# Opening of a one-core transformer kernel: four weight units in one table, split by k, and a shorter run of ones products

## The chip, the cores and the metric

One core of one Trainium2 chip runs the whole kernel. The metric is the device time of one execution in microseconds (us). The kernel before takes 1102.69 us, the median of 3 runs (1102.63 to 1103.09).

## The reference, cut to what matters

A batch of one sequence of 512 positions with 1024 channels goes through two blocks (a gated DeltaNet with retention and a gated MLP, then sliding-window attention with pooling and a long convolution). Only its first step matters here:

```
n = rms_norm(x, attn_norm_w)              # [512, 1024]
proj = n @ w_in                           # w_in is [1024, 4104], float32
gq, gk, gv, gg, ga, gb, rq, ... = split(proj)
```

The kernel works on transposed tiles: 128 channels on the partitions, 512 positions along the free axis. It multiplies x by the norm weight first and applies 1/rms to the products, so that the products needn't wait for the mean of the squares. The mean is needed once the first products are read out.

## The kernel before

**Products in three parts.** A float32 product is made of three float32r products, `w_hi x_hi + w_hi x_lo + w_lo x_hi` (`three`, L1912 to L1916). ScalarE makes the rounded part `hi` of a weight block (`split_hi`, L641 to L655), GpSimd makes the rest `lo = raw - hi` (`split_lo`, L531 to L535; for the very first blocks L545 to L549). Of x, ScalarE makes `hi` (`operand_hi`, L672), VectorE makes `lo` (`operand_lo`, L1223 to L1227).

**Units, halves and buffers.** The weights are taken in units of 128 output columns by all 1024 rows, that is 8 k-blocks of 128 rows. A unit is two halves of 4 k-blocks. The halves of units 0 to 3 are taken as a quad: halves n = 0 to 3 are the first halves (k 0 to 3) of the four units, n = 4 to 7 the second halves. `RAW` holds two slots of float32 weights, each a pair of units (8 k-blocks by 256 columns). `WH` and `WL` hold 4 halves each; half n lies in place n % 4, so half 4 can be written only when half 0 has been multiplied. The semaphore `half_done` says so. One k-block of one unit is 3 products of 128 rows by 512 columns; the four units are 96 of them, and unit 4 follows.

**Order of the opening, TensorE.** After four GpSimd memsets it makes 16 products of a table of ones with itself (L2092 to L2094), whose result nobody reads. Then `two_units` (L1964) runs four times: k 0 to 3 for units 0 and 1, k 0 to 3 for units 2 and 3, then k 4 to 7 for units 0 and 1, then for units 2 and 3. Ahead of the fourth, one float32 product of ones with the summed squares (`stat`, L2061 to L2064) gives the mean for the norm.

**Order of the opening, loads.** ScalarE's queue issues x tiles 0 and 1 (L693). SyncE's queue issues in this order (L382 to L400): norm weights; k 0 and 1 of the first pair of units (L383, 256 KB); k 2 and 3 (L384); x 2 and 3; k 0 to 3 of the second pair (L386, 512 KB); x 4 and 5; k 4 to 7 of the first pair (L388); x 6 and 7; k 4 to 7 of the second pair (L390); then the other parameters, the identity, the small a and b columns, the masks and the cosines. Weight rows are 1 KB long (256 columns), x rows 2 KB. Then the loop of L405 loads pair 2 once `free_slot(2)` holds, that is after 6 `lo` parts (L106 to L108 and L360).

**Order of the opening, ScalarE (L695 to L735).** `hi` of x 0, of weights k 0 and 1 for units 0 and 1 (L711), of x 1, of weights k 2 and 3 (L717), of x 2 and 3; squares of x 0 and 1; halves 2 and 3; x 4 and 5; squares 2 and 3; halves 4 and 5; x 6 and 7; squares 4 and 5; halves 6 and 7; squares 6 and 7; a table load; the two steps to 1/rms; halves 8 and 9.

**Order of the opening, VectorE (L1244 to L1262).** A product of two rows of norm weights (L1246); `lo` of x 0 to 3; sums of squares 0 and 1; `lo` of x 4 and 5; sums 2 and 3; `lo` of x 6 and 7; sums 4 to 7. Squares lie in two buffers in turn, so that square k waits for sum k - 2 (L676).

```
            pe.wait_ge(ones_ready, 4)                                  # L2092
            for _ in range(16):
                mm(PS[:, 7, 0:P], ONES[:, :], ONES[:, :], start=True, stop=True)
```

Of the kernel before, what the change touches and what calls it, by code (L numbers as in the profile page):

```python
# [9 lines left out]
P = 128  # L10
S = 512
D = 1024
KT = D // P
# [92 lines left out]
def split_when_free(p):  # L106

    return 4 * p - 2 if 2 * (p - 2) in QUADS else 4 * (p - 1)  # L108
# [12 lines left out]
def loads_before(p):  # L121

    n = 0
    for q in range(p % 2, p + 1, 2):
        n += 1 if q < 2 else 3 if U6 <= 2 * q < U7 else 2
    return n


def build(nc, a, const, out):
    ctx = ExitStack()  # L130
    with ctx:
# [9 lines left out]
        RAW = at("raw", [P, 2, KT, 256], F32, 0)  # L141
        WH = at("w_hi", [P, 4, 4, P], F32R, 16384)
# [145 lines left out]
        first_in = [sem("first_weights_in0"), sem("first_weights_in1")]  # L288
# [4 lines left out]
        head_in, head_hi, head_lo = sem("head_weights_in"), sem("head_hi_ready"), sem("head_lo_ready")  # L293
# [52 lines left out]
        def f32(ap):  # L346
            return ap.bitcast(F32)
# [7 lines left out]
        def _(sp):  # L355
# [22 lines left out]
            def x_tiles(k0):  # L378
                for k in (k0, k0 + 1):
                    sp.dma_start(XT[:, k, :], a["x"][:, k, :]).then_inc(x_in[k], 16)  # L380

            sp.dma_start(PAR[:, 0:88], a["params"][:, 0:88]).then_inc(par_in, 16)  # L382
            sp.dma_start(RAW[:, 0, 0:2, :], rows(w_in, 0, 2, 512)).then_inc(head_in, 16)  # L383
            sp.dma_start(RAW[:, 0, 2:4, :], rows(w_in, 2 * P, 2, 512)).then_inc(first_in[0], 16)  # L384
            x_tiles(2)
            sp.dma_start(RAW[:, 1, 0:4, :], rows(w_in, 0, 4, 768)).then_inc(first_in[1], 16)  # L386
            x_tiles(4)
            sp.dma_start(RAW[:, 0, 4:8, :], rows(w_in, 512, 4, 512)).then_inc(raw_in[0], 16)  # L388
            x_tiles(6)
            sp.dma_start(RAW[:, 1, 4:8, :], rows(w_in, 512, 4, 768)).then_inc(raw_in[1], 16)  # L390
# [122 lines left out]
        def raw_half(n):  # L513
# [5 lines left out]
            t = u % 2  # L519
            if by_heads(n):  # L520
                return r.rearrange("p k (v t d) -> p k v t d", v=2, t=2)[:, :, :, t, :]
# [8 lines left out]
        def _(gp):  # L530
# [96 lines left out]
        def _(act):  # L627
# [13 lines left out]
            def split_hi(n, i=None):  # L641
# [5 lines left out]
                if n < 4:  # L647
                    act.wait_ge(first_in[p], 16)
                elif i is None:
                    act.wait_ge(raw_in[p % 2], 16 * loads_before(p))  # L650
# [47 lines left out]
            def x_operands(k0):  # L698
                for k in (k0, k0 + 1):
                    act.wait_ge(x_in[k], 16)  # L700
                    operand_hi(XT[:, k, :], XA[:, k, 0, :], vec("attn_norm_w", k))

            def x_squares(k0):
                for k in (k0, k0 + 1):
                    square(0, k, XT[:, k, :], SC[:, 2 + k % 2, :])

            act.wait_ge(x_in[0], 16)
            operand_hi(XT[:, 0, :], XA[:, 0, 0, :], vec("attn_norm_w", 0))
            act.wait_ge(head_in, 16)
            for n in range(2):  # L710
                nc.scalar.activation(WH[:, n, 0:2, :], RAW[:, 0, 0:2, n * P:(n + 1) * P], ACT.Copy) \  # L711
                    .then_inc(head_hi, 1)
            act.wait_ge(x_in[1], 16)
            operand_hi(XT[:, 1, :], XA[:, 1, 0, :], vec("attn_norm_w", 1))
            act.wait_ge(first_in[0], 16)
# [1871 lines left out]
```

## Time and profile before

| | before |
|---|---|
| median of 3 runs | 1102.69 us |
| the profiled execution's own time | 1104.48 us |
| its span | 1102.60 us |
| TensorE busy (share of the span) | 1087.8 us (99%) |
| VectorE busy | 669.3 us (61%) |
| GpSimd busy | 501.0 us (45%) |
| ScalarE busy | 463.9 us (42%) |

The span runs from the first instruction to the last. The profiled execution's own time holds what lies around the span as well, 1.88 us. Its span is 0.09 us under the median. TensorE is busy all along, so what can be won on a stretch is only what TensorE idles or does for nothing in it. A float32 matmul on TensorE is recorded as two instructions, a float32r matmul as one.

### The profile page before, as it was taken

The numbers are of one execution on the slowest core, as the hardware profiler recorded it, in microseconds if no ns is written. First come the engines' busy times: TensorE is split into PE (matmuls) and PEld (weight loads), VectorE is DVE, ScalarE is ACT, GpSimd is POOL, SyncE is SP. The second block draws the span as 40 slices with busy tenths as digits, with TensorE's granted clock in tenths as the row PEclk, the third lists the DMA queues.
The fourth block names the chain that finished last, engine by engine and source line by source line (L and its number), as shares of the span: only waits on it lengthen the run. The fifth ranks groups of instructions, "written<-read, shape, count | busy, mean of one in ns | idle before, by whom it ended". The sixth has DMA issues, their size and how long they took to land.

```text
span 1102.6 us, 16181 instructions
## 1 busy us (share of the span) xinstructions
PE 1087.8 (99%) x5898; PEld 876.4 (79%) x5898; DVE 669.3 (61%) x967; ACT 463.9 (42%) x805; POOL 501.0 (45%) x375
## 2 busy tenths in 40 slices
PE   8999999999999999999999999999999999999997
PEld 7786878788788888888888888877778778888786
DVE  5875886416656666666641222558754757986863
ACT  6436422254744333333333334345464543243663
POOL 4446342122555444444454445433347686632451
PEclk9999999999999999999999999999999999999999
DMA  9952532151222323232322325322115222212222
GB/s 244 136 88 50 64 79 39 58 132 41 77 95 97 115 76 114 76 114 76 114 77 95 105 81 149 114 77 78 39 53 138 56 78 78 77 40 78 77 77 77
DMA packets 101722, 97.29 MB, mean 88 GB/s; under 512 B 4896, under 2 KB 95776, under 8 KB 101280
## 3 DMA queue, kind: packets, MB, share of 16 engines
q1 hardware_dynamic: 101232, 95.71, 31.7%
q8 instruction: 39, 0.64, 0.2%
q10 hardware_dynamic: 432, 0.79, 0.2%
q14 instruction: 19, 0.16, 0.0%
HBM read 94.38 MB, written 2.10 MB: 88 GB/s over the span
## 4 chain that ended last, share of the span: by engine, by line
PE 87%; DVE 7%; ACT 3%; issue 1%; DMA 1%; POOL 1%; SPq 0%; POOLq 0%; DVEq 0%; ACTq 0%
PE ps L1914 25%; PE ps L1916 24%; PE ps L1915 24%; PE ps L2455 4%; PE ps L2118 1%; DVE x_a L1226 1%; DMA raw<-in_w_in 1%; DVE conv L1758 1%; PE ps L2390 1%; PE ps L2401 1%; PE ps L2284 1%; DVE tt L1338 1%; ACT x_a L672 1%; PE ps L2378 1%; POOL w_lo L534 1%
## 5 line engine op out<-in xcount | busy, mean ns | idle before, releaser
L534 POOL TENSOR_TENSOR w_lo<-raw,w_hi 128x512 fp32r<-128x512 f32 (+1 forms) x330 | 447.1, 1365 | 569.5 <-ACT w_hi L655 558.7
L655 ACT ACTIVATE w_hi<-raw 128x512 fp32r<-128x512 f32 (+1 forms) x330 | 201.2, 620 | 254.5 <-PE ps L1916 238.3
L1914 PE MATMUL ps<-x_a,w_hi 128*128 128x512 f32 x624 | 252.2, 404 | 5.8 <-POOL w_lo L534 3.1
L1916 PE MATMUL ps<-x_a,w_lo 128*128 128x512 f32 x624 | 243.5, 390 | 0.0
L1915 PE MATMUL ps<-x_a,w_hi 128*128 128x512 f32 x624 | 243.4, 390 | 0.0
L1914 PE MATMUL ps<-x_b,w_hi 128*128 128x512 f32 x416 | 162.6, 391 | 0.0
L1916 PE MATMUL ps<-x_b,w_lo 128*128 128x512 f32 x416 | 161.9, 389 | 0.0
L1915 PE MATMUL ps<-x_b,w_hi 128*128 128x512 f32 x416 | 161.9, 389 | 0.0
L1914 PEld LDWEIGHTS ps<-x_a,w_hi 128*128 128x128 f32 x624 | 117.2, 188 | 41.0 <-issue 10.6
L1916 PEld LDWEIGHTS ps<-x_a,w_lo 128*128 128x128 f32 x624 | 117.2, 188 | 25.0
L1915 PEld LDWEIGHTS ps<-x_a,w_hi 128*128 128x128 f32 x624 | 117.3, 188 | 24.6 <-issue 2.2
L1914 PEld LDWEIGHTS ps<-x_b,w_hi 128*128 128x128 f32 x416 | 78.1, 188 | 17.5 <-issue 0.8
L1916 PEld LDWEIGHTS ps<-x_b,w_lo 128*128 128x128 f32 x416 | 78.1, 188 | 16.3
L1915 PEld LDWEIGHTS ps<-x_b,w_hi 128*128 128x128 f32 x416 | 78.1, 188 | 16.2 <-issue 0.2
L1758 DVE TENSOR_TENSOR conv<-ps,conv 32x511 f32<-32x511 f32 (+2 forms) x96 | 65.5, 682 | 17.2 <-ACT conv L1100 14.4
L1916 PE MATMUL ps<-mlp_act,w_lo 128*128 128x512 f32 x176 | 68.5, 389 | 0.0
L1915 PE MATMUL ps<-mlp_act,w_hi 128*128 128x512 f32 x176 | 68.5, 389 | 0.0
L1914 PE MATMUL ps<-mlp_act,w_hi 128*128 128x512 f32 x176 | 68.5, 389 | 0.0
L1568 DVE TENSOR_TENSOR ps<-ps,rstd 128x512 f32<-128x512 f32 x44 | 30.7, 698 | 58.3 <-PE ps L1916 53.6
L1593 DVE TENSOR_TENSOR res<-ps,res 128x512 f32<-128x512 f32 x8 | 5.5, 687 | 83.0 <-PE ps L1916 83.0
L935 ACT ACTIVATE mlp_act<-prod_f 128x512 f32 (+1 forms) x22 | 13.9, 632 | 81.2 <-DVE prod_f L1580 81.2
L2455 PE MATMUL ps<-glu_hi,tap_w 32*128 32x512 f32 x512 | 43.2, 395 | 0.0
(348 smaller groups left out, 1520.0 us busy)
## 6 DMA issues: line engine op xcount, KB each, us to landing
raw<-in_w_up SPq DMA_DIRECT2D x44, 512.0 KB, 4.0
raw<-in_w_in SPq DMA_DIRECT2D x31, 512.0 KB, 7.9
raw<-in_c_w_in SPq DMA_DIRECT2D x24, 512.0 KB, 4.7
raw<-in_a_w_in SPq DMA_DIRECT2D x18, 512.0 KB, 4.2
raw<-in_w_down SPq DMA_DIRECT2D x16, 512.0 KB, 4.2
raw<-in_w_out SPq DMA_DIRECT2D x8, 512.0 KB, 4.0
raw<-in_c_w_out SPq DMA_DIRECT2D x8, 512.0 KB, 4.1
raw<-in_w_down SPq DMA_DIRECT2D x8, 384.0 KB, 3.3
```

Source lines behind the costliest of these rows:

```text
L534: nc.gpsimd.tensor_tensor(ring_half(WL, n), raw_half(n), f32(ring_half(WH, n)), SUB) \
L655: nc.scalar.activation(ring_half(WH, n), raw_half(n), ACT.Copy).then_inc(w_hi, 1)
L672: nc.scalar.activation(dst, src, ACT.Copy, scale=scale).then_inc(op_hi, 1)
L935: nc.scalar.activation(ACTS[:, bass.ds(n + (j - 2), 1), 0, :] .rearrange("p a s -> p (a s)"), PRODF[:, j - 2, :], ACT.Copy) \
L1226: v.scalar_tensor_tensor(out=dst_lo, in0=src, scalar=scale, in1=f32(dst_hi), op0=MUL, op1=SUB) \
L1338: ins = v.tensor_tensor(u_, u_, PS[r, 4 + c, 256:256 + P] .rearrange("p (h b s) -> p h b s", h=H, s=s), SUB)
L1568: v.tensor_tensor(x, PS[:, j, :], RSTD[:, :], MUL).then_inc(bank_free, 1)
L1758: ins = v.tensor_tensor(y, PS[32 * q:32 * q + 32, 4 + r, 0:S - late_by], y, ADD)
L1914: mm(out, w_hi_, x_hi_, start=first, stop=False)
L1915: mm(out, w_hi_, x_lo_, start=False, stop=False)
L1916: return mm(out, w_lo_, x_hi_, start=False, stop=last)
L2455: ins = mm(PS[:, 4 + r, :], w, g[p, k % 2, TAP_PHASES * j:TAP_PHASES * j + S], start=first, stop=last)
```

## The change

It touches the first 33 us alone.

- **Loads.** The four units' columns (512 to 1023) are loaded as one table: `RAW8` sees the same bytes of `RAW` as 8 k-blocks by 512 columns, k 0 to 3 in slot 0 and k 4 to 7 in slot 1. Rows are 2 KB long. Four transfers carry one k-block each (256 KB) and two carry two each (512 KB), between single x tiles: norm weights, k 0, k 1, x 2, k 2, x 3, k 3, x 4, x 5, k 4 and 5, x 6, k 6 and 7, x 7. Pair 2 may be loaded after 4 `lo` parts, since slot 0 is then free.
- **Splits.** The first four are made by k: one ScalarE and one GpSimd instruction of 128x512 for each of k 0 to 3, all four units at once. Then halves 4 to 7 as before, by unit.
- **VectorE** makes `hi` of x 0, then waits no more than before for its `lo`; the product of norm weights comes after `lo` of x 3.
- **ScalarE** takes x tiles and weights in turn, puts squares 0 and 1 after `hi` of k 3, square 2 after half 5, square 3 after half 6, and squares 4 to 7 after half 7.
- **TensorE** starts with 9 products of ones, not 16, and after one memset, not four. Then `first_units` goes by k: for k 0 all four `w_hi x_hi`, then all `w_hi x_lo`, then all `w_lo x_hi`, each group with a wait of its own; k 1 for the four units; k 2 and 3 unit by unit; k 4 and k 5 over the four units; k 6 and 7 unit by unit, with `stat` after the first unit's.

```diff
 def split_when_free(p):
-    return 4 * p - 2 if 2 * (p - 2) in QUADS else 4 * (p - 1)
+    return 4 if p == 2 else 4 * p - 2 if 2 * (p - 2) in QUADS else 4 * (p - 1)
...
+            def four_units(k, n, landed):
+                sp.dma_start(RAW8[:, k:k + n, :], w_in[k * P:(k + n) * P, 512:1024]
+                             .rearrange("(k p) c -> p k c", p=P)).then_inc(landed, 16)
...
-            for k, hi, lo in ((0, head_hi, head_lo), (2, w_hi, w_lo)):
-                for n in range(2):
-                    gp.wait_ge(hi, n + 1)
-                    nc.gpsimd.tensor_tensor(WL[:, n, k:k + 2, :], RAW[:, 0, k:k + 2, n * P:(n + 1) * P],
-                                            f32(WH[:, n, k:k + 2, :]), SUB).then_inc(lo, 1)
-            for u in range(1, 14):
+            for k in range(4):
+                gp.wait_ge(w_hi, k + 1)
+                nc.gpsimd.tensor_tensor(WL[:, :, k, :], RAW8[:, k, :].rearrange("p (n c) -> p n c", c=P),
+                                        f32(WH[:, :, k, :]), SUB).then_inc(w_lo, 1)
+            for u in range(2, 14):
                 unit(u)
...
+            first_hi(0)
+            act.wait_ge(op_hi, 1)
+            x_operand(1)
+            first_hi(1)
+            x_operand(2)
+            first_hi(2)
+            x_operand(3)
+            first_hi(3)
             act.wait_ge(x_in[0], 16)
...
+            x_square(0)
+            x_square(1)
+            x_operand(4)
+            x_operand(5)
             split_hi(4)
+            x_operand(6)
             split_hi(5)
-            x_operands(6)
-            x_squares(4)
+            x_square(2)
+            x_operand(7)
             split_hi(6)
+            x_square(3)
             split_hi(7)
-            x_squares(6)
+            for k in range(4, KT):
+                x_square(k)
...
+            dve.wait_ge(x_in[0], 16)
+            v.tensor_scalar(XA[:, 0, 0, :], XT[:, 0, :], vec("attn_norm_w", 0), None, MUL).then_inc(op_hi, 1)
             x_low(0, 4)
+            v.tensor_tensor(p0, p0, fw, MUL)
...
+            def first_units(X):
...
+                pe.wait_ge(w_hi, 1)
+                pe.wait_ge(op_hi, 1)
+                for j in range(4):
+                    mm(PS[:, j, :], WH[:, j, 0, :], X[:, 0, 0, :], start=True, stop=False)
+                pe.wait_ge(op_lo, 1)
+                for j in range(4):
+                    mm(PS[:, j, :], WH[:, j, 0, :], X[:, 0, 1, :], start=False, stop=False)
+                pe.wait_ge(w_lo, 1)
+                for j in range(4):
+                    mm(PS[:, j, :], WL[:, j, 0, :], X[:, 0, 0, :], start=False, stop=False)
+                for k in (1, 2, 3):
+                    pe.wait_ge(w_hi, k + 1)
+                    pe.wait_ge(w_lo, k + 1)
+                    operand(k)
+                    if k == 1:
+                        for j in range(4):
+                            part(1, j)
+                for j in range(4):
+                    part(2, j)
+                    part(3, j).then_inc(half_done, 1)
+                for k in (4, 5):
+                    operand(k)
+                    for j in range(4):
+                        if k == 4:
+                            pe.wait_ge(w_hi, 4 + j + 1)
+                            pe.wait_ge(w_lo, 4 + j + 1)
+                        part(k, j)
+                for j in range(4):
+                    if j == 0:
+                        operand(6)
+                        operand(7)
+                    if j == 1:
+                        stat(0)
+                    part(6, j)
+                    part(7, j, True).then_inc(half_done, 1)
...
-            pe.wait_ge(ones_ready, 4)
-            for _ in range(16):
+            pe.wait_ge(ones_ready, 1)
+            for _ in range(9):
                 mm(PS[:, 7, 0:P], ONES[:, :], ONES[:, :], start=True, stop=True)
```

## Rows read from the trace of the kernel before

**Rows 1.** The page: busy us of each engine, and the chain of waits by engine.

```profile
PE 1087.8 (99%) x5898; PEld 876.4 (79%) x5898; DVE 669.3 (61%) x967; ACT 463.9 (42%) x805; POOL 501.0 (45%) x375
...
PE 87%; DVE 7%; ACT 3%; issue 1%; DMA 1%; POOL 1%; SPq 0%; POOLq 0%; DVEq 0%; ACTq 0%
```

**Rows 2.** Busy time by stretch: length, each engine's busy us, granted clock, DMA share, GB/s.

```profile
7.00:16.00 9.00, 7.10 (x28) 4.95 (x29) 6.10 (x7) 7.22 (x14) 4.98 (x6) 1.00 1.05 350
16.00:32.40 16.40, 16.40 (x72) 13.16 (x71) 12.94 (x15) 9.45 (x15) 9.01 (x6) 1.00 0.97 165
```

**Rows 3.** Timeline of TensorE: start us, length us, what, count [idle before, releaser].

```profile
1.10 4.40 PE L2094 MATMUL ps<-ones 128*128 128x128 f32 x19 [1.10 <-POOL const_bias L544]
...
5.32 1.63 PE L2094 MATMUL ps<-ones 128*128 128x128 f32 x13
6.94 0.47 PE L1914 MATMUL ps<-x_a,w_hi 128*128 128x512 f32 x1
...
14.04 0.47 PE L1914 MATMUL ps<-x_a,w_hi 128*128 128x512 f32 x1 [1.07 <-POOL w_lo L534]
...
15.75 0.47 PE L1914 MATMUL ps<-x_a,w_hi 128*128 128x512 f32 x1 [0.77 <-POOL w_lo L534]
...
26.05 1.02 PE L2064 MATMUL ps<-acc,ones 128*128 128x512 f32 x2
...
32.40 0.39 PE L1914 MATMUL ps<-x_a,w_hi 128*128 128x512 f32 x1
```

**Rows 4.** The chain of waits that ended last, its pieces before TensorE's run.

```profile
3.16 8.74 DMA raw<-in_w_in
11.92 0.64 ACT w_hi L655
12.63 2.98 POOL w_lo L534 x2
```

**Rows 5.** Timeline of ScalarE.

```profile
5.56 0.72 ACT L711 ACTIVATE w_hi<-raw 128x256 fp32r<-128x256 f32 x2 [0.82 <-DMA raw<-in_w_in]
...
27.11 0.69 ACT L688 ACTIVATE rstd<-ps,const_bias 128x512 f32<-128x512 f32 x1 [1.95 <-PE ps L2064]
```

**Rows 6.** Timeline of GpSimd.

```profile
6.06 1.42 POOL L548 TENSOR_TENSOR w_lo<-raw,w_hi 128x256 fp32r<-128x256 f32 x2 [5.01 <-ACT w_hi L711]
...
12.63 1.27 POOL L534 TENSOR_TENSOR w_lo<-raw,w_hi 128x512 fp32r<-128x512 f32 x1 [3.31 <-ACT w_hi L655]
...
17.27 1.74 POOL L534 TENSOR_TENSOR w_lo<-raw,w_hi 128x512 fp32r<-128x512 f32 x1
...
29.06 2.55 POOL L534 TENSOR_TENSOR w_lo<-raw,w_hi 128x512 fp32r<-128x512 f32 x2 [4.72 <-ACT w_hi L655]
```

**Rows 7.** Timeline of VectorE.

```profile
4.77 0.75 DVE L1226 SCALAR_TENSOR_TENSOR x_a<-x_t,params,x_a 128x512 fp32r<-128x512 f32 x1 [0.92 <-ACT x_a L672]
...
17.96 1.60 DVE L1237 TENSOR_TENSOR acc<-acc,scratch 128x512 f32<-128x512 f32 x1
...
25.00 0.69 DVE L1237 TENSOR_TENSOR acc<-acc,scratch 128x512 f32<-128x512 f32 x1
...
70.46 0.70 DVE L1269 TENSOR_TENSOR ps<-ps,rstd 128x512 f32<-128x512 f32 x1 [1.60 <-PE ps L1916]
```

**Rows 8.** Loads: issue on SyncE's queue (L383, then L386), each with its landing.

```profile
L383 SPq DMA_DIRECT2D raw<-in_w_in x1: 418/418/418, 1.2 to 1.2; - x1
...
DMA to landing us min/median/max: 4.3/4.3/4.3
...
L386 SPq DMA_DIRECT2D raw<-in_w_in x1: 433/433/433, 3.2 to 3.2; - x1
...
DMA to landing us min/median/max: 8.7/8.7/8.7
```

**Rows 9.** All DMA from 7 to 8 us, then from 11 to 12 us.

```profile
DMA packets 257, 0.39 MB, mean 394 GB/s; under 512 B 26, under 2 KB 103, under 8 KB 257
...
DMA packets 343, 0.39 MB, mean 386 GB/s; under 512 B 12, under 2 KB 297, under 8 KB 343
```

More of the change, by code:

```diff
@@ L141, in build @@
         RAW = at("raw", [P, 2, KT, 256], F32, 0)
+        RAW8 = RAW[:, :, :, :].rearrange("p s (k two) c -> p (s k) (two c)", two=2)
         WH = at("w_hi", [P, 4, 4, P], F32R, 16384)
@@ L287, in build @@
         x_in = [sem("x_in%d" % k) for k in range(KT)]
-        first_in = [sem("first_weights_in0"), sem("first_weights_in1")]
+        first_in = [sem("first_weights_in%d" % k) for k in range(4)]
         par_in, taps_in = sem("norm_weights_in"), sem("conv_taps_in")
@@ L377, in _, with x_tile @@
             w_in = a["w_in"][0]
-            def x_tiles(k0):
-                for k in (k0, k0 + 1):
-                    sp.dma_start(XT[:, k, :], a["x"][:, k, :]).then_inc(x_in[k], 16)
-            sp.dma_start(PAR[:, 0:88], a["params"][:, 0:88]).then_inc(par_in, 16)
[L383 to L390, printed above, removed]
+            def x_tile(k):
+                sp.dma_start(XT[:, k, :], a["x"][:, k, :]).then_inc(x_in[k], 16)
+            def four_units(k, n, landed):
+                sp.dma_start(RAW8[:, k:k + n, :], w_in[k * P:(k + n) * P, 512:1024]
+                             .rearrange("(k p) c -> p k c", p=P)).then_inc(landed, 16)
+            sp.dma_start(PAR[:, 0:88], a["params"][:, 0:88]).then_inc(par_in, 16)
+            four_units(0, 1, first_in[0])
+            four_units(1, 1, first_in[1])
+            x_tile(2)
+            four_units(2, 1, first_in[2])
+            x_tile(3)
+            four_units(3, 1, first_in[3])
+            x_tile(4)
+            x_tile(5)
+            four_units(4, 2, raw_in[1])
+            x_tile(6)
+            four_units(6, 2, raw_in[1])
+            x_tile(7)
             sp.dma_start(PAR[:, 88:NPAR], a["params"][:, 88:NPAR]).then_inc(taps_in, 16)
@@ L710, in _ @@
[L710 to L715, printed above, removed]
-            for n in range(2):
-                nc.scalar.activation(WH[:, n, 2:4, :], RAW[:, 0, 2:4, n * P:(n + 1) * P], ACT.Copy) \
-                    .then_inc(w_hi, 1)
@@ L719, in _, with x_operand, x_square, first_hi @@
-            x_operands(2)
-            x_squares(0)
-            split_hi(2)
-            split_hi(3)
-            x_operands(4)
-            x_squares(2)
+            def x_operand(k):
+                act.wait_ge(x_in[k], 16)
+                operand_hi(XT[:, k, :], XA[:, k, 0, :], vec("attn_norm_w", k))
+            def x_square(k):
+                square(0, k, XT[:, k, :], SC[:, 2 + k % 2, :])
+            def first_hi(k):
+                act.wait_ge(first_in[k], 16)
+                nc.scalar.activation(WH[:, :, k, :], RAW8[:, k, :].rearrange("p (n c) -> p n c", c=P), ACT.Copy) \
+                    .then_inc(w_hi, 1)
@@ L1962, in four_halves, with part, two_units @@
                     ins.then_inc(half_done, 1)
-            def two_units(q, m, X, k0, j0, fill=None, midway=None):
+            def first_units(X):
+                def part(k, j, last=False):
+                    return three(PS[:, j, :], WH[:, j, k % 4, :], WL[:, j, k % 4, :], X[:, k, 0, :], X[:, k, 1, :],
+                                 False, last)
+                pe.wait_ge(w_hi, 1)
[33 more added lines that the diff above has]
+                    part(7, j, True).then_inc(half_done, 1)
+            def two_units(q, m, X, k0, j0, fill=None):
                 for k in range(4):
-                    if k == 0 and midway is not None:
-                        stat(midway)
                     if fill is not None:
@@ L1975, in two_units @@
                                 pe.wait_ge(bank_free, m + j - 3)
-                            pe.wait_ge(head_hi if n < 2 else w_hi, n + 1)
-                            pe.wait_ge(head_lo if n < 2 else w_lo, n + 1)
-                        if k == 2 and n < 2:
                             pe.wait_ge(w_hi, n + 1)
@@ L1984, in two_units, with unit @@
                             ins.then_inc(half_done, 1)
-            def unit(u, m, X, fill=None, later=None, mlater=None, midway=None, between=None, third=None):
+            def unit(u, m, X, fill=None, later=None, mlater=None, between=None, third=None):
                 for q in QUADS:
@@ L2252, in _ @@
                 else:
-                    unit(u, u, XA, fill=0 if u == 0 else None, midway=0)
+                    unit(u, u, XA, fill=0 if u == 0 else None)
                 if u == 5:
```

26 lines of the change are left out of this document (6 added, 20 removed).

## The prediction

> **What bounds the kernel now.** I read the page first. TensorE is busy 99% of the span and holds 87% of the chain that ended last [rows 1]; there is no second engine near it. So the change can win only where TensorE stands still or does nothing useful, and the busy table by stretch shows where that is: from 7 to 16 us it is busy 7.10 of 9.00 us, from 16 to 32.4 us it has no gap at all [rows 2]. The timeline of TensorE gives the points. Products of ones run from 1.10 to 6.9 us, the first real product starts at 6.94, and after two waits that end on GpSimd (at 14.04 and 15.75) the run is unbroken up to 32.40, where unit 4 begins [rows 3]. The product at 15.75 is the 28th of the 96. I call the start of unit 4 **T**; before, T = 32.40. What moves T moves the end: by 70 us VectorE waits for TensorE again [rows 7], so no chain that began with the statistics is left over that could keep the old time, and the rest of the span is TensorE's. The chain of waits tells why 15.75: the load of the second pair's k 0 to 3 (3.16 to 11.9), then ScalarE's rounding, then two splits on GpSimd [rows 4].
>
> **One product's price.** From 15.75 to 32.40 there are 69 products and the statistics product. The stretch is 16.65 us; the statistics product is two records with 1.02 us between start and end [rows 3], of which I take 0.95 as its place in the stream. (16.65 - 0.95) / 69 = 0.227 us for one product.
>
> **Start of TensorE's real work.** The first 256 KB of weights is issued at 1.2 and lands 4.3 us later, at 5.5 [rows 8]; ScalarE starts on it at 5.56 [rows 5]. In the changed kernel the first k-block has the same size and the same place in the queue, so I leave the landing at 5.5. One rounding of 128x512 takes 0.64 us [rows 4], so w_hi of k 0 is there at about 6.2. `hi` of x 0 goes to VectorE, where an operation of this size costs 0.75 us [rows 7] and is over by 5 us, well under the wait for the weights: cost nothing; with that cover gone it would cost those 0.75 us. TensorE starts at 6.2, not 6.94. The nine products of ones are 18 records at (5.32 - 1.10) / 19 = 0.22 us each [rows 3], 4.0 us from about 1.0, so they end at 5.0 and no longer stand in the way. Their own gain is inside the 0.74 us.
>
> **First phase, k 0 to 3.** TensorE has 12 products for each k-block, 12 x 0.227 = 2.7 us. What it must wait for is GpSimd, which now makes four splits of 128x512 in a row from 6.2 us. A split takes 1.27 us alone and 1.74 where VectorE works between two SBUF tables at the same time [rows 6]; VectorE suffers too, 1.60 against 0.69 us [rows 7]. VectorE has `lo` of x 1 to 3 and two sums in just that stretch, so I take one split at 1.27 and three at 1.74: 6.5 us, and the fourth split is done at 12.7 us. I call the start of the 25th product (k 2, unit 0) **H**; all four splits must be there, so H = 12.7. Bounds: if the splits keep up with TensorE, H = 6.2 + 24 x 0.227 = 11.65. If loads are late, k 3 is the eighth block of 256 KB; before, the eighth block landed at 3.16 + 8.7 = 11.9 [rows 4, 8], and rounding and a split put H at 14.3. I take 12.7 because the DMA engines move as much in rows of 1 KB as in mixed rows (386 GB/s from 11 to 12 us, 394 from 7 to 8 us, [rows 9]), so longer rows alone needn't change much, while the order helps: by bytes, k 3 no longer stands behind blocks that are not needed yet.
>
> The Trainium skill ("SBUF — State Buffer", section "Who interferes with whom") says that GpSimd and VectorE take their shared port pair as an exclusive lock for a whole instruction. By that a contended split would cost 1.27 + 0.69 = 1.96 us, the four 7.2 us, and H would be 13.4; the row of 1.74 us decides for the smaller price.
>
> **Second phase.** From H there are 72 products and the statistics, 16.65 + 3 x 0.227 = 17.33 us, if nothing waits. But halves 4 to 7 go into the places of halves 0 to 3. The first place comes free after 6 products, at H + 1.4, then every 1.4 us. ScalarE adds 0.64 and GpSimd four splits; with two of them contended 2 x 1.27 + 2 x 1.74 = 6.0 us. Half 7 is there at H + 8.1 to H + 8.4, also because ScalarE has two x tiles and two squares between its halves. TensorE asks for it at unit 3's k 4, after 24 products of k 2 and 3 and 9 of k 4: H + 33 x 0.227 = H + 7.5. A new wait of about 0.8 us, price 0 if no split is contended, 1.5 if all are. Before, all waits of the opening together were the 1.90 us that TensorE stood still from 7 to 16 us [rows 2] and some tenths at its first products.
>
> **Statistics.** The squares are later in ScalarE's order. By my count sum 7 ends near 24.5 us on VectorE (each pair of square and sum 0.7 us once GpSimd rests), and `stat` is asked for at H + 13.3 = 26 us: no wait. Behind it: 18 products and itself, about 5.0 us, to T. Before, `stat` began at 26.05, ScalarE's first step at 27.11, and the split of half 8 ran from 29.06 for 1.27 us, to 30.33: 4.3 us from end to end [rows 3, 5, 6]. So unit 4 finds its weights with 0.7 us to spare. If sum 7 slips by more than 1.5 us, that is next.
>
> **Queues.** SyncE has 13 issues where it had 12 for the same bytes, some 0.45 us each [rows 8], but they run 4 us and more ahead of the landing, and pair 2 may now be loaded as soon as the queue is through: costs nothing. ScalarE's wait for `op_hi` is over before its first rounding ends.
>
> **Sum.** T = 12.7 + 17.33 + 0.8 = 30.8 against 32.40: 1.6 us less. The span of the profiled execution, 1102.60, becomes 1101.0 and its own time, 1104.48, becomes 1102.9. The median of the runs is 1102.69, 0.09 over that span, and becomes 1101.1. That is 0.15%. About 0.2%, 2.2 us here, is what a measurement of this kernel can tell from no change, so the forecast is "same", on the faster side.
>
> **Rivals.**
> - *The splits keep up.* H = 11.65 to 12.2 and no wait at half 7: T = 29.0 to 29.7, 1099.3 to 1100.0. For it: a quarter of the work starts with loads that come in the needed order, and w_lo of k 0 is not needed for the first 8 products. Against it: GpSimd's 1.74 us. With the upper part of my own case it makes the chance of a clear gain. 0.30.
> - *Loads still set the pace.* H = 14.3, and T = 31.6 to 33.1: 1101.9 to 1103.4. For it: what held the eighth block back until 11.9 us before may be the time and not the order. Against it: 386 GB/s in that very microsecond [rows 9]. 0.13.
> - *TensorE stays at 1.2 GHz.* The records show the clock rise at 5.32 us: before, 19 records of ones take 4.22 us, after, 13 take 1.62 us, 0.22 and 0.125 us each, the levels of 1.2 and 2.4 GHz, after 4.2 us of unbroken work [rows 3]. Nine products of ones end at 5.0 us, before that point, and TensorE then rests for 1.2 us. If the clock rises late, a product costs 0.454 us until then. With H set by GpSimd at 12.7, a rise up to 8.3 us costs nothing; from there on each us costs half a us. At 11.5 us the whole gain is gone. If k 0 to 3's first 24 products all run slowly, H = 6.2 + 24 x 0.454 = 17.1, T = 34.4 to 35.2, and the time is 1104.7 to 1105.5: the case on the slower side. Chance 0.05, and it takes part of the case before with it. The Trainium skill ("TensorE: Matmul & The Clock Gate", section "What you observe") puts the change of clock around 4 us into sustained matmul activity, with 500 ns from run to run; by that rule nine products are at the edge.
> - *It does not do what it says*: statistics or pair 2 turn out late and give the gain back, T = 32.4, 1102.7. 0.04. My own case holds the remaining 0.48.
>
> **Chances and range.** Faster by over 0.2%: the 0.30 and 0.06 of my own case, 0.36. Slower by over 0.2%: 0.05. Within: 0.59. The range is 1099.5 (splits nearly keep up) to 1103.0 (loads late); it leaves out the slow clock and the ends of both neighbours.
>
> **What would show it.** TensorE's first real product near 6.2 us; four splits of 128x512 on GpSimd without pause, the last done near 12.7, and TensorE's wait before the 25th product released by GpSimd; a second wait of under 1 us before unit 3's k 4; T near 30.8. Wrong would be: the rounding of k 3 released by a load after 11 us; products of 0.4 us and more spacing after 8.3 us; a wait of `stat` for VectorE; or T under 29.7.

## The result and the profile after

The changed kernel takes 1104.7 us, the median of 18 runs (1104.0 to 1106.3), beside 1102.73 us for the kernel before (18 runs): ratio 1.0018 (1.0012 to 1.0025). It is slower by 2.0 us, under the 0.2% that I took as the least a measurement can tell, but its interval leaves no change out. It is "same" by the 0.2% that I had set, as forecast, but it moved the wrong way and lies outside my range of 1099.5 to 1103.0, on the side to which I gave almost nothing. The profiled execution after has a span of 1102.4 us and an own time of 1104.67.

**First a correction to the reading of before.** I set the profiled span of before, 1102.60, beside the median of the runs, 1102.69. Over 33 later runs of the kernel before the median span is 1100.9 us and the time around it 1.89: the profiled execution was 1.7 us longer than usual. It held a wait of 0.81 us at 149.5 us that other profiles of the same kernel don't have, and its T, 32.40 [rows 3], is 31.89 in experiment 1 and 31.81 and 32.11 in the same instructions with other layouts of the inputs (experiments 15 and 7). The fair comparison is span 1100.9 against 1102.45 (+1.55 us) and time around the span 1.89 against 2.27 us (+0.38), together 1.9 of the 2.0 us.

The page of the kernel after, which answers to [rows 1]:

```profile
PE 1087.2 (99%) x5884; PEld 875.7 (79%) x5884; DVE 671.4 (61%) x968; ACT 462.8 (42%) x802; POOL 500.4 (45%) x373
...
PE 87%; DVE 5%; ACT 3%; DMA 2%; issue 1%; POOL 1%; SPq 0%; POOLq 0%; DVEq 0%; ACTq 0%
```

TensorE still holds the chain. Its busy time by stretch, as in [rows 2]:

```profile
7.00:16.00 9.00, 9.00 (x36) 7.28 (x35) 8.20 (x8) 6.05 (x12) 5.89 (x4) 1.00 1.07 360
16.00:32.40 16.40, 15.65 (x66) 12.01 (x65) 10.81 (x12) 11.38 (x18) 8.11 (x6) 1.00 0.95 160
```

The first stretch has no hole any more, where before was idle for 1.90 us; the second has one of 0.75 us. TensorE's timeline after (as [rows 3]) places it:

```profile
1.00 4.21 PE L2137 MATMUL ps<-ones 128*128 128x128 f32 x18 [1.00 <-POOL const_bias L552]
6.47 2.07 PE L1982 MATMUL ps<-x_a,w_hi 128*128 128x512 f32 x4 [1.26 <-ACT w_hi L713]
...
13.44 0.39 PE L1923 MATMUL ps<-x_a,w_hi 128*128 128x512 f32 x1
...
22.10 0.47 PE L1923 MATMUL ps<-x_a,w_hi 128*128 128x512 f32 x1 [0.75 <-POOL w_lo L543]
...
26.99 1.02 PE L2107 MATMUL ps<-acc,ones 128*128 128x512 f32 x2
...
31.97 0.39 PE L1923 MATMUL ps<-x_a,w_hi 128*128 128x512 f32 x1
...
144.37 0.47 PE L1923 MATMUL ps<-x_a,w_hi 128*128 128x512 f32 x1 [1.55 <-POOL w_lo L543]
```

T is 31.97, where I had 30.8; against the 31.81 to 32.11 that other profiles of the kernel before show, the opening wins nothing. The last line is new: a wait of 1.55 us at 144 us, a place at which my prediction never looked, and as long as the span grew. The chain of waits of the kernel after leads to it from a load:

```profile
125.09 0.37 SPq L374
125.50 14.78 DMA raw<-in_w_in
140.30 0.64 ACT w_hi L661
141.01 3.22 POOL w_lo L543
144.37 0.47 PE ps L1923
```

The same load of the kernel before (the second half of a pair, k 4 to 7, issued at 125.4) takes 13.5 us, and TensorE doesn't wait. The view of the loads of 120 to 132 us, first of the kernel after:

```profile
L374 SPq DMA_DIRECT2D raw<-in_w_in x2: 368/438/508, 125.1 to 125.5; - x2
...
DMA to landing us min/median/max: 8.5/11.6/14.8
```

and then of the unchanged kernel, profiled again:

```profile
L374 SPq DMA_DIRECT2D raw<-in_w_in x2: 368/438/508, 125.0 to 125.4; - x2
...
DMA to landing us min/median/max: 8.8/11.1/13.5
```

The same line issues the same bytes at the same time, and they land 1.3 us apart. So there were three questions: why the opening won nothing, what lengthens this load 90 us behind the change, and what the 0.38 us outside the span are.

### The profile page after: what moved, and what is told of

Its sections match the earlier page's. It is cut to its first block, busy times and chain, and to the rows that moved or that the text cites. A ratio compares the mean times of both kernels' runs of the same rounds, so it can differ in the third digit from the quotient of the medians.

```text
span 1102.4 us, 16149 instructions
## 1 busy us (share of the span) xinstructions
PE 1087.2 (99%) x5884; PEld 875.7 (79%) x5884; DVE 671.4 (61%) x968; ACT 462.8 (42%) x802; POOL 500.4 (45%) x373
## 4 chain that ended last, share of the span: by engine, by line
PE 87%; DVE 5%; ACT 3%; DMA 2%; issue 1%; POOL 1%; SPq 0%; POOLq 0%; DVEq 0%; ACTq 0%
PE ps L1923 25%; PE ps L1925 24%; PE ps L1924 24%; PE ps L2498 4%; DMA raw<-in_w_in 2%; POOL w_lo L543 1%; PE ps L2161 1%; DVE x_a L1233 1%; DVE conv L1767 1%; PE ps L2433 1%; PE ps L2444 1%; PE ps L2327 1%; DVE tt L1347 1%; ACT x_a L678 1%; PE ps L2421 1%
## 5 line engine op out<-in xcount | busy, mean ns | idle before, releaser
L1923 PEld LDWEIGHTS ps<-x_a,w_hi 128*128 128x128 f32 x620 | 116.5, 188 | 39.8 <-issue 12.7
L1924 PEld LDWEIGHTS ps<-x_a,w_hi 128*128 128x128 f32 x620 | 116.5, 188 | 24.5 <-issue 2.2
```

The lines of the kernel that those rows point to most:

```text
L1923: mm(out, w_hi_, x_hi_, start=first, stop=False)
L1924: mm(out, w_hi_, x_lo_, start=False, stop=False)
```

## The experiments

They ran in four groups, each on one chip with runs of the kernel before beside it, which gave medians of 1102.70 to 1102.83 us. T, waits and loads are read from one profiled execution of each experiment. "The kernel before" and "the changed kernel" name what was edited.

**1. The kernel before again.** No edit.

> The kernel before, unchanged, profiled again. Theory A (the profiled execution of before was a slow draw: its own time, 1104.48 us, lies 1.79 us over the median): this profile's own time is within 0.7 us of the median, and T, the start of unit 4, is near 30.6 us and not 32.40. Theory B (what lies around the span varies, the span is as it was): T stays within 0.3 us of 32.40 and the time around the span is near 0.1 us to 1.0 us instead of 1.88. Ratio to before 1.000 either way.

Measured: 1102.84 us (11 runs), ratio 1.0000 (0.9991 to 1.0009). T = 31.89, span 1101.0; no wait near 144 or 149 us. This is what showed that the profile of before was no usual one, though T did not fall to the 30.6 that theory A had named.

**2. The changed kernel again.** No edit.

> The changed kernel again, for pairing on the same chip: 1.5 to 2.5 us over before. If the loss were a matter of the chip it ran on, the ratio would be within 0.0005 of 1.

Measured: 1105.13 us (11 runs), ratio 1.0022 (1.0013 to 1.0031). T = 32.23, and the same wait of 1.55 us at 144.61. The first four products took 1.20 us, not 2.07, which didn't bring T forward (see experiment 4). ScalarE began half 4 at 15.56, when its load landed, 2.5 us after H.

**3. The shorter run of ones alone, on the kernel before.**

```diff
-            for _ in range(16):
+            for _ in range(9):
```

> The kernel before with 9 products of ones, not 16: that part of the change alone. Clock theory: the products end near 5.1 us, the rise to 2.4 GHz comes late (near 9 us, as in the profile after), and the opening, with two units at a time and its loads as before, loses 1.0 to 2.0 us. Load theory (loads and splits set T, TensorE's clock is hidden): less than 0.4 us from before.

Measured: 1103.13 us (11 runs), ratio 1.0004 (0.9995 to 1.0013), T = 32.05. TensorE stood still for 2.04 us ahead of its first product, at 7.28, and its clock fell later. Busy time by stretch, where the number behind PE's, PEld's, DVE's, ACT's and POOL's is the granted clock:

```profile
9.00:10.00 1.00, 1.00 (x4) 0.81 (x3) 1.00 (x1) 1.00 (x2) 0.66 (x1) 0.50 0.94 281
...
12.00:13.00 1.00, 1.00 (x6) 0.83 (x5) 0.01 (x1) 1.00 (x3) 0.72 (x1) 1.00 1.07 378
```

From 9 to 11 us the granted clock was 0.50, the level of 1.2 GHz. T hardly felt it: from 7.28 to T TensorE waited for nothing, and the slow products filled time in which it waits for splits elsewhere (0.28 and 0.76 us in experiment 15, where T is 31.81).

**4. The longer run of ones, on the changed kernel.**

```diff
-            for _ in range(9):
+            for _ in range(16):
```

> The changed kernel with 16 products of ones again. Clock theory: TensorE starts 0.7 us later but at 2.4 GHz, the first 24 products take 5.5 us instead of 6.9, and the kernel gains 0.5 to 2 us over the changed one. Load theory: half 4 to 7 wait for the load of k 6 and 7 (landed at 15.3 us in the profile after), so T and the time stay within 0.4 us of the changed kernel.

Measured: 1105.08 us (11 runs), ratio 1.0022 (1.0013 to 1.0031). TensorE's timeline:

```profile
6.52 1.20 PE L1982 MATMUL ps<-x_a,w_hi 128*128 128x512 f32 x4 [0.33 <-ACT w_hi L713]
...
13.29 0.47 PE L1923 MATMUL ps<-x_a,w_hi 128*128 128x512 f32 x1 [0.69 <-POOL w_lo L556]
...
22.42 0.47 PE L1923 MATMUL ps<-x_a,w_hi 128*128 128x512 f32 x1 [0.76 <-POOL w_lo L543]
```

All products are quick, so TensorE now stands still before the 25th, released by GpSimd, which was hidden in the profile after. Slow products had filled that wait and some 0.2 us more: the 25th starts 0.35 us after the fourth split ends here and in experiment 2, and 0.55 us after it in the profile after. T is 32.25; the 9 or 16 ones make no difference to it here.

**5. The changed kernel with the loads of before** (two and four k-blocks in rows of 1 KB; all else, the splits by k too, as changed).

```diff
-            four_units(0, 1, first_in[0])
-            four_units(1, 1, first_in[1])
+            two_units_in(0, 2, 0, first_in[0])
+            two_units_in(2, 2, 0, first_in[1])
             x_tile(2)
-            four_units(2, 1, first_in[2])
             x_tile(3)
-            four_units(3, 1, first_in[3])
+            two_units_in(0, 4, 1, first_in[2])
             x_tile(4)
             x_tile(5)
-            four_units(4, 2, raw_in[1])
+            two_units_in(4, 4, 0, raw_in[1])
             x_tile(6)
-            four_units(6, 2, raw_in[1])
             x_tile(7)
+            two_units_in(4, 4, 1, raw_in[1])
```

> The changed kernel, but with the loads of before (1 KB rows, the same seven transfers in the same order into the new table), so that the first product has to wait for the second pair's k 0 to 3. Opening: first product near 12.5 us, T (start of unit 4) near 36 us, all theories. The stall of 1.55 us near 144 us, where half of a unit waits for a load that takes 14.8 us in the changed kernel and 13.5 us before: theory L (the loads of the opening leave something behind that slows later loads) expects 13.5 us and no stall over 0.5 us; theory P (where the tensors and the program lie in memory differs between the two builds) expects 14.8 us and the stall still there.

Measured: 1108.65 us (3 runs), ratio 1.0053 (1.0030 to 1.0076). The first product starts at 11.04, where I had expected 12.5, and T is 37.5, where I had 36. So splits by k need loads by k. The load at 131 us took 13.7 us and TensorE didn't wait for it. That is what theory L had said (the loads of the opening leave something behind) and not what theory P had (the place in memory, tested in experiments 7 to 9): the inputs lay where they did in the changed kernel.

**6. The changed kernel with two k-blocks in a load.**

```diff
-            four_units(0, 1, first_in[0])
-            four_units(1, 1, first_in[1])
+            four_units(0, 2, first_in[0])
             x_tile(2)
-            four_units(2, 1, first_in[2])
+            four_units(2, 2, first_in[1])
             x_tile(3)
-            four_units(3, 1, first_in[3])
```

> The changed kernel with its 2 KB rows, but two k-blocks in a transfer from the start (8 transfers for weights and parameters fewer by 2). T within 1 us of the changed kernel (32.0 to 33). If the number of transfers counts for the later load: 13.5 us and no stall; if row length or placement count: 14.8 us and the stall of 1.5 us stays.

Measured: 1106.94 us (5 runs), ratio 1.0035 (1.0019 to 1.0051), T = 34.4, later than I had expected. The load near 125 us took 14.7 us and the wait is there (1.53 us, at 146.81). TensorE's first three groups, then GpSimd's first:

```profile
7.67 2.08 PE L1980 MATMUL ps<-x_a,w_hi 128*128 128x512 f32 x4 [2.46 <-ACT w_hi L711]
9.54 1.91 PE L1983 MATMUL ps<-x_a,w_hi 128*128 128x512 f32 x4
11.24 1.91 PE L1986 MATMUL ps<-x_a,w_lo 128*128 128x512 f32 x4
```

```profile
7.69 6.36 POOL L554 TENSOR_TENSOR w_lo<-raw,w_hi 128x512 fp32r<-128x512 f32 x4 [6.64 <-ACT w_hi L711]
```

After 2.46 us at rest TensorE made all 12 products of k 0 at some 0.45 us each. The splits were done at 14.05, but TensorE only came to the 25th product at 16.05. With 0.3 us for the handing over, that is the slow-clock rival at work with 1.7 us, and without them T would be 32.7 by this estimate, inside what was expected. Experiment 5 shows it too, after a rest of 5.83 us (groups of 2.07, 1.91 and 1.91 us), with some 1.3 us by the same working. The profile's granted clock reads 1.00 in both stretches; that these products ran at 1.2 GHz is read from their pace, four in a microsecond, which is the pace of experiment 3 where the granted clock reads 0.50. Neither was run again with 16 ones. In the changed kernel TensorE starts earlier and rests less, and the rival costs little there.

**7 and 8. The weight matrix elsewhere in memory.** The same instructions, with `w_in` last among the large inputs; on the kernel before, and on the changed kernel.

```diff
-    x = {name: np.ascontiguousarray(inputs[name]) for name in _AS_GIVEN}
+    x = {name: np.ascontiguousarray(inputs[name]) for name in _AS_GIVEN[1:] + _AS_GIVEN[:1]}
```

> The kernel before with w_in as the last of the large input tensors rather than the first: only its place in memory differs. Theory P: the landing time of the load at 125 us moves away from 13.5 us (by over 0.5 us, either way) and the time with it. Theory L: 13.5 us within 0.2, time within 0.5 us of before.

Measured on the kernel before: 1103.41 us (8 runs), ratio 1.0005 (0.9993 to 1.0016); load 13.8 us, no wait at 144.

> The changed kernel with w_in as the last of the large input tensors. Theory P: the load at 125 us moves away from 14.8 us, and if it gets under 13.8 us the stall near 144 us is gone and the kernel is 1 to 1.5 us faster than the changed one. Theory L: 14.8 us and the stall stay.

Measured on the changed kernel: 1104.02 us (8 runs), ratio 1.0009 (0.9998 to 1.0020). The load takes 13.5 us and the wait at 144 is gone, but the median is only 0.7 to 1.1 us under that of the changed kernel, and T was later, 33.16: in this profile, the slowest of the eight runs, halves 4 to 7 came late three times (19.95, 21.63 and 23.32 us), not once, after ScalarE had stood still for 3.39 us for the load of k 6 and 7, up to 16.55. So the order of the inputs goes with 14.8 or 13.5 us in the changed kernel, and experiment 9 tests it again.

**9. The changed kernel with `x` put ahead of `w_in`** (another shift, as a second test of the placement).

```diff
-    x = {name: np.ascontiguousarray(inputs[name]) for name in _AS_GIVEN}
+    x = {"x": np.ascontiguousarray(inputs["x"][0].T.reshape(KT, P, S).transpose(1, 0, 2))}
+    x.update({name: np.ascontiguousarray(inputs[name]) for name in _AS_GIVEN})
```

> The changed kernel with x (2 MB) ahead of w_in among the inputs, so that w_in lies elsewhere again. Placement theory: landing of the load near 125 us is again one of the two values seen so far, 13.5 or 14.8 us, and the stall near 144 us is there with 14.8 and not with 13.5. If landing and stall are as in the changed kernel, moving by 2 MB does not matter.

Measured: 1103.12 us (10 runs), ratio 1.0002 (0.9993 to 1.0012); load 13.5 us, no wait at 144, T = 31.94. Its median span is 1100.85, that of the kernel before: with the wait gone nothing of the 1.55 us is left, and the opening wins nothing. The time around the span stays at 2.27. The profiled execution was the slowest of the ten, with a span of 1102.2. TensorE has another wait in it, 1.28 us at 833.56 us, which no other profile of these experiments has; ahead of it ScalarE had stood still for 5.33 us for a load of `ab_w_out`:

```profile
833.56 0.47 PE L1923 MATMUL ps<-x_b,w_hi 128*128 128x512 f32 x1 [1.28 <-ACT w_hi L661]
```

**10. Squares later on ScalarE, in the changed kernel.**

```diff
             split_hi(5)
-            x_square(2)
             x_operand(7)
             split_hi(6)
-            x_square(3)
             split_hi(7)
-            for k in range(4, KT):
+            for k in range(2, KT):
                 x_square(k)
```

> The changed kernel with squares 2 and 3 moved on ScalarE from between halves 5 to 7 to behind half 7. Theory S (in the second phase ScalarE's order holds back halves 6 and 7): hi of half 7 comes 1.0 us sooner, the wait before unit 3's k 4 falls from 0.75 to 0.2 us or less and T from 32.2 to about 31.6 us. Rival (GpSimd's splits and the load of k 6 and 7 at 15.3 us set it): T within 0.2 us of 32.2; the sums come later and stat may wait.

Measured: 1104.85 us (10 runs), ratio 1.0018 (1.0008 to 1.0028). The wait at 22.1 is gone, one of 0.31 us at 21.45 is left, and another has come:

```profile
21.45 0.47 PE L1921 MATMUL ps<-x_a,w_hi 128*128 128x512 f32 x1 [0.31 <-POOL w_lo L543]
27.03 1.12 PE L2105 MATMUL ps<-acc,ones 128*128 128x512 f32 x2 [0.56 <-DVE acc L1242]
```

`stat` now waits for VectorE's sums, and T is 32.08, no better. The splits and the statistics both lie within half a us of the path; moving the squares trades one for the other. The 31.6 that theory S had named was missed.

**11. All eight k-blocks by k** (on the changed kernel: ScalarE and GpSimd split k 4 to 7 as they do k 0 to 3, each into place k % 4 once that k has been multiplied; k 4 and 5 have a semaphore of their own; TensorE goes over the four units for k 0 to 5; squares 2 and 3 ahead of x 6; 13 ones).

```diff
-            four_units(4, 2, raw_in[1])
+            four_units(4, 2, first_in[4])
...
             x_operand(4)
+            first_hi(4)
             x_operand(5)
-            split_hi(4)
-            x_operand(6)
-            split_hi(5)
+            first_hi(5)
             x_square(2)
-            x_operand(7)
-            split_hi(6)
             x_square(3)
-            split_hi(7)
+            x_operand(6)
+            first_hi(6)
+            x_operand(7)
+            first_hi(7)
...
-                for k in (1, 2, 3):
+                for k in range(1, 6):
```

> The changed kernel with all eight k-blocks of the four units split and multiplied by k (k 4 and 5 need only their own load, k 6 and 7 only theirs), and 13 products of ones. Theory D (halves 4 to 7 wait for the load of k 6 and 7, since a half holds k 4 to 7): TensorE runs unbroken from k 1 on, T near 30.5 us, 1.7 us under the changed kernel, and the time 1103.4 if the stall near 144 us stays. Rival (GpSimd's eight splits set the pace anyway, or stat waits for the sums on VectorE): T 31.5 to 32.5 us.

Measured: 1103.67 us (10 runs), ratio 1.0009 (0.9999 to 1.0018). No wait for a split is left up to `stat`, but `stat` waits 1.27 us for VectorE at 25.85, unit 4 waits 0.55 us for its split at T = 31.62, and the wait at 144 is there (1.54 us; the load took 14.8). ScalarE stood still for 2.07 us for the load of k 4 and 5 and took k 4 at 14.48; in experiments 12 and 16 it took it at 13.00 and 12.53. The profiled execution was a long one: its span is 1102.4, beside a median of 1101.4 and 1100.6 to 1105.5 in the ten runs, so how often these waits come is not shown.

**12. The same with `w_in` last** (the edit of experiment 7).

> The same with w_in as the last of the large inputs in memory. Placement theory: the load near 125 us lands in 13.5 us instead of 14.8, the stall of 1.5 us near 144 us is gone, and the time is 1.0 to 1.6 us under the same kernel with w_in first: near 1102. Otherwise equal to it.

Measured: 1101.73 us (10 runs), ratio 0.9990 (0.9980 to 0.9999); load 13.4 us, no wait at 144, `stat` at 25.50 after 0.39 us, T = 30.59. The gain over experiment 11 is 1.9 us, of which the wait at 144 is 1.54 in the profiles; the rest goes with the opening.

**13. Only the small parts, on the kernel before** (`hi` of x 0 on VectorE, the product of norm weights after `lo` of x 3, ones after one memset, 9 ones).

```diff
-            act.wait_ge(x_in[0], 16)
-            operand_hi(XT[:, 0, :], XA[:, 0, 0, :], vec("attn_norm_w", 0))
...
+            dve.wait_ge(x_in[0], 16)
+            v.tensor_scalar(XA[:, 0, 0, :], XT[:, 0, :], vec("attn_norm_w", 0), None, MUL).then_inc(op_hi, 1)
...
-            pe.wait_ge(ones_ready, 4)
-            for _ in range(16):
+            pe.wait_ge(ones_ready, 1)
+            for _ in range(9):
```

> The kernel before with the change's small parts alone: x 0 rounded on VectorE, the product of norm weights later, 9 products of ones after one memset. Of the 0.38 us by which the time around the span has grown (1.89 to 2.27 us in every build with the new opening): if one of these parts makes it, it is 2.2 us here; if the loads or the new products make it, 1.9 us. T within 0.4 us of 32.0, time within 0.5 us of before apart from that. Placement theory: w_in as in before, so the load near 125 us takes 13.5 us.

Measured: 1102.80 us (8 runs), ratio 1.0003 (0.9993 to 1.0013). Time around the span 1.89, load 13.5 us, no wait at 144, T = 31.63. The small parts do nothing that the time shows, and nothing around the span.

**14. One more transfer, on the kernel before** (the load of 512 KB at L386 as two of 256 KB).

```diff
-            sp.dma_start(RAW[:, 1, 0:4, :], rows(w_in, 0, 4, 768)).then_inc(first_in[1], 16)
+            for k in (0, 2):
+                sp.dma_start(RAW[:, 1, k:k + 2, :], rows(w_in, k * P, 2, 768)).then_inc(first_in[1], 16)
```

> The kernel before with the load of the second pair's k 0 to 3 in two transfers of 256 KB, 13 instead of 12 transfers ahead of the parameters. If the number of transfers makes the time around the span longer, it is 2.1 us or more; otherwise 1.9. Opening and time as before within 0.5 us.

Measured: 1102.75 us (8 runs), ratio 1.0000 (0.9990 to 1.0011). Load 13.4 us. The time around the span rose to 2.02 us, 0.13 more (1.99 to 2.06, where the kernel before has 1.84 to 2.01 with a median of 1.89). That is a third of the 0.38 us.

**15. The kernel before with `x` ahead** (the edit of experiment 9).

> The kernel before with x ahead of w_in among the inputs. Placement theory: the landing of the load near 125 us is one of the two values, 13.5 or 14.8 us; if 14.8, the stall near 144 us appears in the kernel before too, and it is 1 to 1.5 us slower than before. A value in between, or a stall at 13.5, would speak against it.

Measured: 1102.81 us (8 runs), ratio 1.0002 (0.9991 to 1.0012), load 13.6 us, time around the span 1.91. No change of the kernel before can be told in either order that was tried, though its median with `w_in` last was 0.6 us higher.

**16. All by k, with `x` ahead** (experiment 11 with the edit of experiment 9).

> The version by k with x ahead of w_in. As in the changed kernel with x first, the load near 125 us should land in 13.5 us and the stall near 144 us be gone: 1.0 to 1.6 us under the version by k with w_in first (1103.7), so 1102.1 to 1102.7. That the gain of the version by k over the changed one with the same placement (1103.1) stays, 0.7 to 1.5 us, shows what the opening itself is worth.

Measured: 1101.22 us (10 runs, 1101.0 to 1101.7), ratio 0.9987 (0.9977 to 0.9997): faster than both kernels, by 1.5 us than before, and 0.9 us under the 1102.1 that I had expected at best. GpSimd's timeline:

```profile
6.20 6.40 POOL L556 TENSOR_TENSOR w_lo<-raw,w_hi 128x512 fp32r<-128x512 f32 x4 [5.15 <-ACT w_hi L718]
13.24 5.09 POOL L556 TENSOR_TENSOR w_lo<-raw,w_hi 128x512 fp32r<-128x512 f32 x3 [0.64 <-ACT w_hi L718]
18.53 1.50 POOL L556 TENSOR_TENSOR w_lo<-raw,w_hi 128x512 fp32r<-128x512 f32 x1 [0.21 <-ACT w_hi L718]
```

and TensorE's:

```profile
24.95 1.12 PE L2106 MATMUL ps<-acc,ones 128*128 128x512 f32 x2 [0.42 <-DVE acc L1249]
...
30.02 0.39 PE L1928 MATMUL ps<-x_a,w_hi 128*128 128x512 f32 x1
```

The eighth split is done at 20.03, where the changed kernel had it at 21.97, T is 30.02, and the load near 123 us takes 13.7 us. Against experiment 15, the same layout, T is 1.8 us earlier, and 0.35 of it goes to the time around the span, which is 2.26: 1.45 of the 1.59 us measured between the two.

## Why the prediction was wrong, by its steps

I forecast 1101.1 us and measured 1104.7. The 3.6 us between them are three pieces: the opening's gain of 1.6 us did not come (T is 1.17 us later than forecast, and the usual T of before is 0.3 to 0.6 us earlier than the 32.40 that I started from); TensorE waits 1.55 us at 144 us; and 0.38 us came around the span.

**Start at 6.2.** Right within 0.3: 6.47 and 6.25 in two profiles, 6.52 with 16 ones. ScalarE began at 5.79, 0.23 later than in [rows 5], as the first load landed later by that.

**First phase, H = 12.7.** Right in kind and nearly in size. GpSimd's timeline of the kernel after:

```profile
6.50 6.39 POOL L556 TENSOR_TENSOR w_lo<-raw,w_hi 128x512 fp32r<-128x512 f32 x4 [5.45 <-ACT w_hi L713]
16.01 2.56 POOL L543 TENSOR_TENSOR w_lo<-raw,w_hi 128x512 fp32r<-128x512 f32 x2 [3.12 <-ACT w_hi L661]
18.81 3.15 POOL L543 TENSOR_TENSOR w_lo<-raw,w_hi 128x512 fp32r<-128x512 f32 x2 [0.24 <-ACT w_hi L661]
```

Four splits took 6.39 us where I had 6.5. They began 0.3 us late and ended at 12.89; with 0.35 us of handing over to TensorE, for which the sum had nothing, H was 13.05 and 13.29 in two profiles, and 13.44 in the profile after, with the 0.2 us of slow products on top. Experiment 4 shows the wait that I named for it, released by GpSimd. The price of 7.2 us for the four that I worked out from the Trainium skill ("SBUF — State Buffer", section "Who interferes with whom") is above what ran.

**Second phase: the step that failed in the opening.** I let half 4 begin when its place came free, at H + 1.4, and had half 7 ready at H + 8.1 to 8.4. But a half holds k 4 to 7 of one unit, so even the first of them needs the last load. I priced that load at nothing because its issue ran ahead, and the place comes free later than I had it. The chain of waits after, and ScalarE's line:

```profile
6.38 8.89 DMA raw<-in_w_in
15.30 0.63 ACT w_hi L661
15.93 0.47 ACT x_a L678
16.45 0.63 ACT w_hi L661
17.08 0.52 ACT scratch L684
17.76 0.36 issue
18.12 0.62 ACT w_hi L661
18.81 3.16 POOL w_lo L543 x2
```

```profile
15.30 0.63 ACT L661 ACTIVATE w_hi<-raw 128x512 fp32r<-128x512 f32 x1 [2.57 <-DMA raw<-in_w_in]
```

ScalarE stood still for 2.57 us and began half 4 at 15.30, 1.2 us behind my H + 1.4 = 14.1. Most of that is not the load's: 0.74 us is H. In experiment 9 the load was no longer what came last, and the free place was:

```profile
15.17 0.63 ACT L661 ACTIVATE w_hi<-raw 128x512 fp32r<-128x512 f32 x1 [2.45 <-PE ps L1925]
```

There H was 13.55, so the place was usable at H + 1.6 and not at H + 1.4, and T was 31.94, as here. By that the load held half 4 back by some 0.2 us in the profile after, by 0.6 to 0.9 us in experiments 2, 4 and 10, and by 1.8 us in experiment 8; these are estimates. "Queues: costs nothing" was the sentence that let the load by, and the place was the other half of the step.

The eighth split ended at 21.97, where I had 20.8 to 21.1. GpSimd rested 3.12 us between its fourth and fifth split; in experiment 16 it rests 0.64 us. There k 4 needs only the load of k 4 and 5, and a place that is free once k 0 has been multiplied, so the experiment takes away both causes and can't tell them apart. T is 1.17 us above the forecast: 0.74 from H, and 0.43 from this phase, whose waits and slips come to 1.2 us (31.97 - 13.44 - 17.33) and not 0.8. What was left to win is counted against a T of before of 31.8 to 32.1, not against the 32.40 of one unusual profile: that takes the last 0.3 to 0.6 us of the 1.6, and the gain is gone.

**Statistics.** `stat` began at 26.99 with no wait, as said, but the slack was small: sum 7 ended at 26.16, where I counted 24.5. Experiments 10 and 16 show VectorE as the next to be waited for.

**What no step had: the load at 125 us.** This cost as much as the opening's miss. I said that the rest of the span is TensorE's, and so put every other cost there at nothing. The kernel before had in that rest a load of 13.3 to 13.5 us whose slack was smaller than 1.3 us, and I never asked how much slack the loads behind the change had. Where the load takes 14.7 to 15.0 us, TensorE waits 1.53 to 1.55 us (six profiles); where it takes 13.3 to 13.8, nothing (twelve profiles). Changing the order of the inputs alone turns the one into the other in the changed kernel (8, 9) and in the kernel by k (11 against 12 and 16). That the layout of the inputs is part of the cause is thus shown, with one profile of each build; the addresses themselves were not recorded. It is not the whole cause. The six profiles with the late landing all have the new opening's loads, in rows of 2 KB, and the first layout; with the loads of before (the kernel before in three layouts, experiment 5) the load was quick each time. Why it takes both is open. The rest of the +1.97 us, 0.38 outside the span, is not in the profile at all: one more transfer, tried on the kernel before, accounts for 0.13, the small parts for nothing, the rest is open.

**The rivals.** "The splits keep up" fell: TensorE waits for GpSimd at the 25th product. "Loads still set the pace" was wrong as I put it (the eighth block came in time, and ScalarE took k 3 at 9.82 with no wait), yet a load had a part in the pace of the second phase, which I had not thought of. "TensorE stays at 1.2 GHz": four products took 2.07 us in the profile after, 1.20 in the next. All twelve of k 0 took 4.25 us and 3.13 us, so products at half pace lasted beyond the 8.3 us up to which the case had them for nothing; they cost 0.2 us of H and nothing that T shows (31.97 against 32.23). With a later start they did cost 1.7 us in experiment 6. The page's rule (the Trainium skill, "TensorE: Matmul & The Clock Gate", section "What you observe") puts nine products at the edge. That fits a start that is quick in one execution and slow in another, behind 4.21 us of ones in both, and gives no other time here. "It does not do what it says" held T = 32.4 and 1102.7 us: the opening did end without a gain, but at T = 31.97 and beside a usual T of before that is no later, and the loss came from elsewhere. No case of mine held a cost behind T, and that is why 0.05 stood for slower.

## What to carry to other kernels

This kernel, whose bounding engine is 99% busy, had a place with next to no slack 90 us behind the change. Before a change at its opening is priced, look through its long loads for those that land just in time, and judge none of it by one profiled execution, whose span may be 1.7 us off the usual. A block that is consumed whole is ready when its last piece lands; to win from loads that come by k, splits and products must go by k as far as they are loaded so. And time a few layouts of the inputs beside each version: the same instructions differed here by 0.7 to 2.5 us for the order of the inputs, in the kernels with the new opening.

## What the runs showed that I had not expected

- **A landing that hangs on the layout of the inputs.** One strided load of 512 KB takes 14.7 to 15.0 or 13.4 to 13.8 us in the same instructions by where `w_in` lies among the inputs. Together with the other half of its pair it comes slowly in either case. All DMA from 125.5 to 134 us, of the kernel after and then of the kernel before in experiment 1, and last of the kernel after from 138.8 to 140.3 us:

```profile
DMA packets 648, 0.65 MB, mean 76 GB/s; under 512 B 16, under 2 KB 648, under 8 KB 648
...
DMA packets 701, 0.70 MB, mean 83 GB/s; under 512 B 16, under 2 KB 701, under 8 KB 701
...
DMA packets 435, 0.44 MB, mean 296 GB/s; under 512 B 17, under 2 KB 434, under 8 KB 434
```

In these two profiles the rate is lower from the start, by a tenth, as the load is longer by a tenth. From 138.8 us, with the next pair's loads under way, rows of the same 1 KB come at 296 GB/s; the opening had 386 to 394 [rows 9]. What makes this pair slow wasn't tried.
- **The time around the span is not a constant of the chip.** It is 1.89 us in the kernel before, 2.02 with one more transfer at its start, 2.13 in experiment 6 and 2.15 in experiment 5, and 2.23 to 2.29 in every build with the new opening and its loads.
- **Ones and clock.** With nine products of ones and 1.0 to 1.6 us of rest, the first four real products take 1.20 us in one execution and 2.07 in another; with 2.46 and 5.83 us of rest all twelve of k 0 were slow; with 16 ones, and with 13, none was. The granted clock of the profile reads 1.00 in the slow stretches as well. In the kernel before with nine ones (experiments 3 and 13) the first products were quick and the granted clock fell to 0.50 from 9 to 11 us. The clock clearly moved T in experiments 5 and 6 alone; in experiment 9, where half 4 waited for TensorE, it may have cost up to 0.4 us.
